# Moving the products with the gates from VectorE to GpSimd in a hybrid attention block

## What is computed

```python
h = _rmsnorm(x, pre_norm[l]);  proj = h @ w_in[l]        # split into the groups and the gate
# diff:   softmax(q0 k0 + bias) - lam * softmax(q1 k1 + bias), times v, then
o_a = _rmsnorm(o_a, diff_head_norm[l]) * (1.0 - lam_init)  # one root per row
# stick:  sigmoid weights with a running product over keys, times v (needs no division)
# forget: softmax(q k * scale + c_q - c_k) times v          # divided by the row's sum z
# mem:    softmax(q km * scale) times vm, over 256 keys     # divided by z
y = jnp.concatenate([o_a, o_b, o_c, o_m], axis=-1)
y = y * jax.nn.silu(gate)
x = x + _rmsnorm(y @ w_out[l], post_norm[l])
```

## Time and profile before

| what | value |
|---|---|
| median of 3 runs | 2684.25 us |
| the profiled execution, its own time | 2690.5 us |
| span of its instructions | 2688.4 us |
| TensorE, busy share of the span | 90% |
| VectorE | 65% |
| ScalarE | 61% |
| GpSimd | 49% |

### The profile page before, as it was taken

How to read it: one execution, slowest core, us unless ns; L and a number is a source line. 1 busy time by engine, 2 the same in 40 slices (tenths; PEclk the granted TensorE clock), 3 DMA queues, 4 the chain that set the end, 5 groups by cost and what they waited for, 6 DMA issues and landing times. The chain is left out here.

```text
span 2688.4 us, 73361 instructions
## 1 busy us (share of the span) xinstructions
PE 2428.3 (90%) x27422; PEld 1657.4 (62%) x27422; DVE 1759.7 (65%) x4673; ACT 1632.8 (61%) x4565; POOL 1324.7 (49%) x2064
## 2 busy tenths in 40 slices
PE   5699999998899999998999999889899998599998
PEld 4576666665676666666766666667666666344443
DVE  7654668977566699885656998865559988411111
ACT  5455887756566888565678885655678866311121
POOL 6412645576656555775565556765655555300000
PEclk9799999999899999999999999999999999699999
DMA  6346898854568898645698886455898864563331
GB/s 197 101 102 117 154 157 152 143 117 80 126 142 171 151 156 146 133 97 118 143 170 155 151 148 128 98 133 127 161 167 141 151 112 83 154 185 100 91 110 47
DMA packets 942748, 357.30 MB, mean 133 GB/s; under 512 B 768420, under 2 KB 927148, under 8 KB 942380
## 3 DMA queue, kind: packets, MB, share of 16 engines
q1 hardware_dynamic: 935800, 334.77, 63.3%
q0 software_dynamic: 6592, 17.83, 2.3%
HBM read 89.16 MB, written 35.23 MB: 46 GB/s over the span
## 5 line engine op out<-in xcount | busy, mean ns | idle before, releaser
L1530 POOL TENSOR_TENSOR rows<-rows 128x512 f16<-128x512 f32 (+3 forms) x864 | 864.8, 1018 | 775.4 <-ACT rows L1461 770.2
L1290 PE MATMUL job<-big,wt 128*128 128x512 f16 x2688 | 680.5, 383 | 12.8 <-DVE planes L1541 5.3
L1290 PE MATMUL job<-wt,big 128*128 128x128 f16 x10752 | 665.9, 219 | 8.4 <-DVE gate_s L1618 5.8
L1290 PEld LDWEIGHTS job<-wt,big 128*128 128x128 f16 x10752 | 625.2, 98 | 56.6 <-DVE gate_s L1618 7.5
L1461 ACT CAST rows<-rows 128x512 f16<-128x512 f32 (+3 forms) x864 | 456.5, 549 | 187.2 <-DMA rows<-rows 102.6
L1477 ACT ACTIVATE rows<-rows,neg_max 128x512 f32<-128x512 f32 (+3 forms) x704 | 447.1, 637 | 133.8 <-DVE neg_max L1587 130.8
L1351 PEld LDWEIGHTS mixed<-values,rows 128*128 128x128 f16 x8544 | 380.0, 99 | 224.1 <-DMA rows<-rows 102.8
L1351 PE MATMUL mixed<-values,rows 128*128 128x64 f16 (+1 forms) x8544 | 432.6, 202 | 91.0 <-DMA rows<-rows 68.4
L1579 DVE TENSOR_SCALAR_CACHE_REDUCE rows<-scores 128x512 f32<-128x512 f32 (+3 forms) x704 | 400.1, 588 | 149.2 <-PE scores L1336 107.7
L1336 PE MATMUL scores<-stack 128*128 128x512 f16 (+3 forms) x1600 | 437.2, 353 | 56.2 <-DVE rows L1579 40.0
L1290 PEld LDWEIGHTS job<-big,wt 128*128 128x128 f16 x2688 | 246.1, 99 | 248.1 <-issue 15.8
(11 more groups left out here) (157 smaller groups left out, 2940.4 us busy)
## 6 DMA issues: line engine op xcount, KB each, us to landing
stack<-planes SPq DMA_DIRECT2D x160, 192.0 KB
ws<-w_in SPq DMA_DIRECT2D x56, 512.0 KB, 4.7
y_halves<-y_out_halves SPq DMA_DIRECT2D x64, 256.0 KB, 2.8
rows<-rows SPq DMA_TRANSPOSE x864, 3.3
rows<-x SPq DMA_DIRECT2D x16, 512.0 KB, 5.3
temps<-w_out POOLq DMA_DIRECT2D x64, 128.0 KB, 3.4
out_weight_halves<-temps POOLq DMA_DIRECT2D x64, 128.0 KB, 3.4
planes<-y_halves SPq DMA_DIRECT2D x8, 1024.0 KB, 8.4
```

The source lines that it names most:

```text
L1290: last = nc.tensor.matmul(dst, lhs, rhs, start=(k0 == 0 and q == 0), stop=(k1 == KT and q == len(pairs) - 1))
L1530: nc.gpsimd.tensor_tensor(halves_of(tau, 1, w), scored(plan.chunk_at(g, m, k0), 0, w), halves_of(tau, 0, w), ALU.subtract).then_inc(low_po ...
```

## The change

- GpSimd multiplies by the gate in all units (`post` on the POOL queue). In diff units it takes two instructions: o_copy times the root, then times the gate. The queue "post" now also holds the roots, in the order of the steps, and has the rank that the roots had (2.48, behind "lo" with 0.59).
- In forget and mem units VectorE takes 1/z (`norm`) as soon as the exponentials are there, before the take. ScalarE's take multiplies by 1/z, in forget units with two instructions of 64 columns. In mem units the sum over one part is left out.
- The planner knows the new work, takes longer for "hi" on ScalarE (0.09 + 0.83 ns a column for 0.10 + 0.58 ns, with a lag of 0.1 for 0.2), and never lets two of the works in `PORT` run at the same time on GpSimd and VectorE. All other numbers and `RANK` are as they were. Since every list comes from the planner, all engines' lists are ordered anew.

```diff
+PORT = ("lo", "wo", "post", "combine", "widen")
-    "dve": {"weigh": -0.70883, "lo_dve": 1.60978, "low": 2.79308, "combine": 2.90619, "post": 5.81204,
+    "dve": {"weigh": -0.70883, "lo_dve": 1.60978, "low": 2.79308, "combine": 2.90619, "norm": 5.81204,
...
-    "pool": {"lo": 0.59157, "root": 2.47661, "wo": 9.04735},
+    "pool": {"lo": 0.59157, "post": 2.47661, "wo": 9.04735},
...
-                q["hi"].append((("hi", tau), ("hi", g, ch), [ready] + split, 0.10 + w * 0.00058, 0.2))
+                q["hi"].append((("hi", tau), ("hi", g, ch), [ready] + split, 0.09 + w * 0.00083, 0.1))
...
             q["take"].append((("take", g), ("take", g), [("mix", self.t_chunks[g][-1][0])]
-                              + ([("post", g - 1)] if g else []), 0.17, 0.1))
+                              + ([("post", g - 1)] if g else []) + ([("norm", g)] if kind in ("forget", "mem") else []),
+                              0.35 if kind == "forget" else 0.19, 0.1))
...
-                q["root"].append((("root", g), ("root", g), [("variance", g)], 3.35, 0.0))
+                q["post"].append((("root", g), ("root", g), [("variance", g)], 3.35, 0.0))
...
             q["post"].append((("post", g), ("post", g), done,
-                              {"stick": 0.22, "forget": 0.9, "mem": 0.75, "diff": 0.3}[kind], 0.08))
+                              0.8 if kind == "diff" else 0.45, 0.08))
...
                     at = max(at, free[e])
+                    if name in PORT:
+                        at = max(at, port)
...
                     if op == "take":
                         act.wait_ge(pv_done, mixed(g))
                         if g:
-                            act.wait_ge(post_step, POST_AT[g])
-                        nc.scalar.activation(o_copy[:, :], o_bank[:, 0:P], ACT.Copy, scale=0.5 / W_SCALE) \
-                            .then_inc(o_copied, 1)
+                            act.wait_ge(posted, g)
+                        heads = {"forget": 2, "mem": 1}.get(KINDS[g], 0)
+                        if heads:
+                            act.wait_ge(norm_done, NORM_AT[g])
+                            wide = P // heads
+                            for h in range(heads):
+                                s = slice(h * wide, (h + 1) * wide)
+                                last = nc.scalar.activation(o_copy[:, s], o_bank[:, s], ACT.Copy,
+                                                            scale=rz[:, g % 2, h:h + 1])
+                        else:
+                            last = nc.scalar.copy(o_copy[:, :], o_bank[:, 0:P])
+                        last.then_inc(o_copied, 1)
...
+                def post(g):
+
+                    kind = KINDS[g]
+                    y, gate = y_f[:, g % 2, :], gate_s[:, g % 2, :]
+                    if g >= 2:
+                        pool.wait_ge(j_full, plan.y_job[g - 2][0] + 1)
+                    pool.wait_ge(j_free, plan.gate_job[g][0] + 1)
+                    pool.wait_ge(o_copied, g + 1)
+                    if kind == "diff":
+                        pool.wait_ge(root_step, (DIFF_STEP[g] + 1) * ROOT)
+                        nc.gpsimd.tensor_scalar(y, o_copy[:, :], root[:, 0:1], None, ALU.mult).then_inc(scaled_y, 1)
+                        pool.wait_ge(scaled_y, DIFF_STEP[g] + 1)
+                        nc.gpsimd.tensor_tensor(y, y, gate, ALU.mult).then_inc(posted, 1)
+                    else:
+                        nc.gpsimd.tensor_tensor(y, o_copy[:, :], gate, ALU.mult).then_inc(posted, 1)
...
+                def norm(g):
+
+                    heads = 2 if KINDS[g] == "forget" else 1
+                    r = 2 * g % ROWS
+                    dve.wait_ge(probs_ready, soft_count(plan.last_of(g, heads - 1) + 1))
+                    if g >= 2:
+                        dve.wait_ge(o_copied, g - 1)
+                    if heads == 2:
+                        sum_rows(g, heads).then_inc(norm_done, 1)
+                        dve.wait_ge(norm_done, NORM_AT[g] - 1)
+                    sums = z_sum[:, r:r + heads] if heads == 2 else z_part[:, r, 0:1]
+                    nc.vector.reciprocal(rz[:, g % 2, 0:heads], sums).then_inc(norm_done, 1)
```

More of the change, by code:

```diff
@@ L227, in low_on_dve, with read_before @@
         return every and tau % every == 0
+    def read_before(self, g):
+        if g < 0 or self.kinds[g] == "stick":
+            return []
+        return [("variance" if self.kinds[g] == "diff" else "norm", g)]
     def queues(self):
@@ L396, in run @@
         free["sp"] = 0.6
-        engines = 0.0
+        engines = port = 0.0
         opened, done, jobs, part = None, 0.0, 0, 0
@@ L484, in run @@
             end[key], on[key] = at + length + lag, e
+            if name in PORT:
+                port = at + length
             if name in DMA_TIME:
@@ L1064, in build @@
         j_full, j_hi, j_free = (sem(n) for n in ("j_full", "j_hi", "j_free"))
-        squared, var_ready, root_step, post_step = (
-            sem(n) for n in ("squared", "var_ready", "root_step", "post_step"))
+        squared, var_ready, root_step, norm_done, posted = (
+            sem(n) for n in ("squared", "var_ready", "root_step", "norm_done", "posted"))
+        scaled_y = sem("scaled_y")
         y_stored = [sem(f"y_stored{b}") for b in range(2)]
@@ L1098, in build @@
         COEF = 3
-        POST = {"stick": 1, "forget": 3, "mem": 3, "diff": 2}
-        VAR, ROOT = 3, 12
-        POST_AT, total = {}, 0
+        VAR, ROOT = 4, 12
+        NORM_AT, total = {}, 0
         for g in range(N_G):
-            POST_AT[g] = total
-            total += POST[KINDS[g]]
+            total += {"stick": 0, "forget": 2, "mem": 1, "diff": 0}[KINDS[g]]
+            NORM_AT[g] = total
         Y_GROUPS = N_G // 4
```

61 lines of the change are left out of this document (20 added, 41 removed).

## The result

The changed kernel takes 2725.85 us (median of 4 runs, 2720.05 to 2728.37) against 2688.64 for the kernel before on the same chip (4 runs, 2683.04 to 2699.21): a ratio of 1.0135, 95% interval 1.0112 to 1.0158. I had forecast 2668 us and a range of 2622 to 2725. The time lies just above the range, and on the side to which I gave 0.24.

A forecast was written before the change was run, and what follows sets the result against it. It took TensorE to bound mem and forget units, three nearly full resources the stick units, and a take-product-mix loop the diff units. -16 - 21 + 21 = -16 us gave a 2668 us median, 8-in-10 range 2622 to 2725.

The forecast's parts named there:

- term 6: All engines: the lists made anew by the planner, taken as 0, bounds -20 and +20 us.
- terms 2 and 3: GpSimd gains 150 us of products, covered by idle time in forget and stick units; the diff units' loop saves 21 us.
- Term 4: Diff units: "lo" and output-weight work that GpSimd's list puts between root and product, +21 us, bounds 0 and +42.
- Term 1: VectorE loses 165.7 us of products; in stick units half the relief counts, -16 us, bounds -32 and 0.
- Term 1's zeros for mem and forget: Mem and forget units: VectorE's relief hidden behind TensorE, taken as 0, bound -4 us a forget unit.
- term 5: Forget units: ScalarE's take has one more instruction in 64 steps, taken as 0, bound +4 us a unit.
- C: GpSimd stands at a product waiting for the take while "lo" queue behind it: 2742 us, chance 0.24.
- its sign of longer waits of mixes for transposes: TensorE: mixes would wait longer for transposes, alongside hundreds of GpSimd waits for o_copy; no size given.
- B: Both reliefs come in full, stick units -32 us and diff loops -21 us: 2627 us, chance 0.32.
- D: GpSimd and VectorE only trade the wait, so gains vanish with the cost of inserted work: 2684 us, chance 0.09.

The follow-up runs named there:

- e5: Kernel before with its lists kept, all products moved from VectorE's list to GpSimd's, in diff units right behind the root: ratio 1.0165 to the kernel before.
- e10: Kernel before with lists kept, only the diff products on GpSimd right behind the root, 1/z ahead of the take: ratio 1.0150.
- e11: Kernel before, products still on VectorE, three fills of an unread tile on GpSimd behind each root: ratio 1.0162.
- e7: Kernel before with lists kept, all products on GpSimd, diff products standing where VectorE's were due, not right behind the root: ratio 1.0140.
- e6: Changed kernel's lists on every engine, 1/z ahead of the take, but the products in VectorE's list: ratio 1.0133 to the kernel before.
- e12: Kernel before with lists kept, only the stick products on GpSimd, 1/z ahead of the take: ratio 0.9966.
- e16: Kernel before with lists kept, stick products on GpSimd, 1/z ahead of the take, root of nine instructions for twelve: 2675.31 us, ratio 0.9940.
- e9: Kernel before with lists kept, mem, forget and stick products on GpSimd, diff products on VectorE, 1/z ahead of the take: ratio 0.9994.
- e18: Changed planner rules and 1/z ahead of the take, but planned and run with all products on VectorE, lists made anew: ratio 1.0138 to the kernel before.
- e1: Changed kernel with the planner's old rules (old length of hi, no PORT): ratio 1.0123 to the kernel before.
- e4: Changed kernel without PORT in the planner, the new length of hi kept: ratio 1.0140 to the kernel before.
- e8: Kernel before with planner number HOP 0.160 for 0.152, which remakes the lists and changes nothing else: ratio 1.0050.
- e17: Changed kernel planned and run with the diff products on VectorE, the others on GpSimd, lists made anew: ratio 1.0139 to the kernel before.
- e13: Kernel before with lists kept, each root nine GpSimd instructions for twelve by a fused tensor_scalar: ratio 0.9971.

## Why the prediction was wrong

Two steps failed. In the kernel as it was changed it was term 6, the new lists taken at 0: they alone lose what was measured. The move by itself failed at terms 2 and 3: with the lists held fixed it loses as much, where I had a gain.

- **Terms 2 and 3, the step that failed for the move itself.** "It is bound by a loop" was right in 33 of the 44 steps, in which the next take starts within 0.15 us of the product ("nearly all" was too much), but the loop that I named was one of two. I wrote that GpSimd's idle times "in forget and stick units" cover its new work, and in the diff units costed it only on the way from root to take: a gain of 21 us. The other loop, root, "lo", next root, was GpSimd's own list, and I read its slack from a window of the whole unit, 115.7 of 164 us. Between the roots of steps 0 to 10 it was 84% full. With the lists kept the moved diff products cost 43 to 44 us (e5, e10) instead of giving 21. The path from the root's end to the product's end took 1.55 us in e5, for 1.64 before and the 1.16 that I had computed: the gap had a mean of 0.36 us and the pair of instructions took 1.19. In the changed kernel it is 2.53. But its length wasn't what counted: e11 has 1.08 us there and loses as much as e10.
- **Term 4** (+21, "lo" between root and product) cost nothing that the runs show. e7 has such work in 36 of the 44 steps and isn't slower than e5, which has none. Single places do look costly. In the last diff unit of the changed kernel:

```profile
2315.72 0.58 POOL L1522 TENSOR_TENSOR root<-root 128x1 f32<-128x1 f32 x1
2316.38 4.20 POOL L1571 TENSOR_TENSOR rows<-rows 128x512 f16<-128x512 f32 x4
2320.57 0.60 POOL L1535 TENSOR_SCALAR y_f<-o_copy,root 128x128 f32<-128x128 f32 x1
2321.25 0.46 POOL L1537 TENSOR_TENSOR y_f<-y_f,gate_s 128x128 f32<-128x128 f32 x1
```

```profile
2322.07 0.27 ACT L1491 COPY o_copy<-mixed 128x128 f32<-128x128 f32 x1 [3.67 <-POOL y_f L1537]
```

  Four "lo" and the product take 5.3 us, and the take waits 3.67 of them. But e6, on the same lists with the product on VectorE, is no faster, so on these lists it costs nothing that shows in the sum either.
- **Term 1** (-16 in stick units) was mis-sized. e12 moves no other products than the stick ones and gives 9.5 us in its median (ratio 0.9966). But it also has 1/z ahead of the take, which no run has alone on the old lists. Of the 9.5 us, 5.9 are in the stick windows. These are 3 to 6 us shorter in e10 and e11, too, which don't touch them, and 2 us longer in e16, which moves the same products. So the windows don't show that the move gained anything in the stick units, and my "half" was too much. A slip in its sum changes nothing: 128 x 0.495 is 63.4, and the 58.2 of the row is its busy time with overlaps counted once.
- **Term 1's zeros for mem and forget and term 5**: e9 moves these as well as the stick products and is 0.28% (about 8 us) slower than e12. Not covered in full, but inside term 5's bound of 4 us a unit. The bound's own length was too small: a take of 64 columns took 309 ns in the changed kernel, where I had 276 as the most.
- **Term 6, the step that failed in the changed kernel** (new lists, 0, bounds -20 and +20), was wrong by the bound. The new lists cost 36 us by e6 (1.0133 x 2688.64 - 2688.64), and e18 has the same. I took a sixth of the waits in the earlier trace rows as a measure of what an order can move; it can make new ones. Eight sets of lists made anew (the change's, e1 to e4, e8, e17, e18), with the products on either engine, were all slower, by 0.5 to 1.4%.
- **The rivals.** C was the nearest in its time, and its sign of longer waits of mixes for transposes came true (68.4 to 85.5 us). But its price isn't what the runs show. GpSimd does stand at products, 53.6 us where C had 37, in 42 waits and not hundreds. The kernel with the lists kept and all products moved stands there as long (e5, 49.9 us), and its forget and stick units aren't longer for it than before. SP's waits for "lo" even fell, from the 979.6 us of the earlier trace rows to 811.4. B's gain in the loops is excluded by e5 with the lists kept; e1, on lists of its own, has diff units 15 us shorter. D's balance is met only by e9 and only outside the diff units. The Trainium skill (Perfetto Trace Analysis, "Optimizing Scalar/DVE Operations"), by which moving work between the two might not help, was the better guide: the trace agrees, with 43 us lost in e10, for a reason that the rule doesn't name, the receiving engine's list.
- **The total.** The +37 us of the change are not the sum of 44 for the move and 36 for the lists. On the changed kernel's lists, where GpSimd idles 139 us between the roots without the products, the move is free. That I gave 0.24 to the right side of the range, by C, was no foresight: C's mechanism isn't the one.

SP's queue in the changed kernel (waits, us, times, longest), for the last point but one:

```profile
SPq L1265 <- POOL rows L1571: 811.4, 515, 13.0
...
SPq L1264 <- PE mixed L1367: 128.8, 45, 8.1
```

## What to carry to other kernels

Before moving work to an engine that looks idle, measure its idle time between the two events of the loop that you want to shorten, step by step, and not over the stage. An engine that runs its list in order and owns a part of a second loop passes on what you add, here about half, even where nobody waits for the added instruction itself; a dummy load of the same length on the unchanged kernel prices this before anything is moved. When an order comes from a planner, hold the lists fixed to price an edit, and make them anew with a neutral change to see how much they alone are worth.

## What the runs showed of the hardware

- On GpSimd a tensor_scalar on one column with two column operands took 430 and 350 ns, against 234 for one with constants. Three instructions less a root, at 0.27 us from start to start, promised 0.8 us; 0.29 came (e13).
- GpSimd's 128-column products took 476 and 503 ns with two inputs in float32, and 650 with one input and a column operand: the form that reads less was the slower one.
- A fill of 380 columns took 414 ns on GpSimd, and VectorE's product beside it 0.35 us (e11, at 1127.48 of the trace), not the 1.25 that it took beside a "lo". The 64 products of e11 took 0.38 us in the mean, against 0.82 before: a fill, which reads nothing, doesn't shut VectorE out.
